# Strassen's seven products for all pairs of projection tiles of a hybrid attention layer

## What is computed

```python
h = jnp.einsum('bsd,de->bse', x, w_in) + b_in            # 1024 x 1024 @ 1024 x 5376
q_a, k_a, v_a, gate_a, q_b, k_b, v_b, gate_b, mg_a, mg_b = jnp.split(h, split_points, axis=-1)
o_a = swa_sink_attention(rope(q_a), rope(k_a), v_a, sinks) * silu(gate_a)   # 8 heads, window of 2 chunks of 64
o_b = stick_breaking_attention(q_b, k_b, v_b) * silu(gate_b)                # 8 heads, causal, 128-query blocks
merged = sigmoid(mg_a) * (o_a @ w_up_a) + sigmoid(mg_b) * (o_b @ w_up_b)
out = layer_norm(alpha * x + merged @ w_out, ln_g, ln_b)
```

## Time and profile before

| what | us |
| --- | --- |
| median of 3 runs (lowest, highest) | 805.31 (802.58, 805.39) |
| the profiled execution, its own time | 805.12 |
| its span | 803.4 |
| PE busy | 782.4 |
| DVE busy | 425.3 |
| ACT busy | 371.9 |
| POOL busy | 241.8 |

### The profile page before, as it was taken

One profiled execution on the slowest core, in us unless ns is written; L12 is line 12 of the kernel. 1 busy time (PEld: TensorE's weight loads), 2 busy tenths in 40 slices (PEclk: granted clock), 3 DMA queues, 4 the chain that ended last, 5 costly groups with the idle time before them and its releaser, 6 DMA issues.

```text
span 803.4 us, 10295 instructions
## 1 busy us (share of the span) xinstructions
PE 782.4 (97%) x4088; PEld 617.3 (77%) x4088; DVE 425.3 (53%) x518; ACT 371.9 (46%) x628; POOL 241.8 (30%) x177
## 2 busy tenths in 40 slices
PE   7999999999999999999999999989999999999996
PEld 6888778778677777777777777768887888888884
DVE  6377555534445445554444667934166367670543
ACT  7688555552555545454554544543546012140221
POOL 0221111112433222322223333455453122200592
PEclk9999999999999999999999999989999999999999
DMA  9231000011001000000004123241515533441261
GB/s 318 76 106 53 26 27 27 27 53 53 27 28 51 27 28 27 26 29 26 28 27 157 56 102 131 80 159 52 170 40 187 206 129 119 173 157 53 93 209 66
DMA packets 25199, 68.85 MB, mean 86 GB/s; under 512 B 2880, under 2 KB 2880, under 8 KB 25152
## 3 DMA queue, kind: packets, MB, share of 16 engines
q1 hardware_dynamic: 25152, 68.20, 24.6%
HBM read 54.55 MB, written 12.58 MB: 84 GB/s over the span
## 4 chain that ended last, share of the span: by engine, by line
PE 89%; DVE 5%; ACT 2%; issue 1%; DMA 1%; POOL 0%; SPq 0%; DVEq 0%; POOLq 0%
PE ps L168 25%; PE ps L170 24%; PE ps L169 24%; PE ps L1415 5%; PE ps L1444 4%; PE ps L1431 4%; PE ps L1360 2%; PE ps L1343 1%; PE ps L1371 1%; DVE xs L1111 1%; DVE t_ops L1094 1%; DMA x_f<-in_xt 1%; DMA raw<-in_w 1%; DVE keep_big L1052 1%; DVE x_lo L1094 0%
## 5 line engine op out<-in xcount | busy, mean ns | idle before, releaser
L168 PE MATMUL ps<-x_hi,w_hi 128*128 128x512 f32 x640 | 262.6, 410 | 6.2 <-DVE x_lo L1094 3.3
L170 PE MATMUL ps<-x_hi,w_lo 128*128 128x512 f32 x640 | 252.3, 394 | 0.0
L169 PE MATMUL ps<-x_lo,w_hi 128*128 128x512 f32 x640 | 251.3, 393 | 0.0
L489 POOL TENSOR_TENSOR w_lo<-raw,w_hi 128x1024 fp32r<-128x1024 f32 x33 | 80.4, 2436 | 296.6 <-ACT w_hi L556 296.6
L168 PEld LDWEIGHTS ps<-x_hi,w_hi 128*128 128x128 f32 x640 | 121.2, 189 | 45.7 <-issue 19.2
L170 PEld LDWEIGHTS ps<-x_hi,w_lo 128*128 128x128 f32 x640 | 121.1, 189 | 27.0
L169 PEld LDWEIGHTS ps<-x_lo,w_hi 128*128 128x128 f32 x640 | 121.7, 190 | 22.3
L1052 DVE TENSOR_TENSOR_SCAN keep_big<-keep_big 128x1025 f32<-128x1025 f32 (+3 forms) x32 | 61.4, 1962 | 63.4 <-POOL keep_big L504 63.4
L168 PE MATMUL ps<-t_ops,w_hi 128*128 128x512 f32 x136 | 53.9, 396 | 1.7 <-POOL w_lo L495 1.7
L170 PE MATMUL ps<-t_ops,w_lo 128*128 128x512 f32 x136 | 53.4, 392 | 0.0
L169 PE MATMUL ps<-t_ops,w_hi 128*128 128x512 f32 x136 | 52.9, 389 | 0.0
(11 more groups left out here) (171 smaller groups left out, 1247.7 us busy)
## 6 DMA issues: line engine op xcount, KB each, us to landing
raw<-in_w SPq DMA_DIRECT2D x42, 512.0 KB, 3.3
sig_d<-sig_m SPq DMA_DIRECT2D x32, 256.0 KB, 2.2
sig_m<-sig_d SPq DMA_DIRECT2D x16, 512.0 KB, 4.2
o_t<-in_xt SPq DMA_DIRECT2D x16, 256.0 KB, 6.2
raw<-in_xn SPq DMA_DIRECT2D x8, 512.0 KB, 3.6
out<-o_t SPq DMA_DIRECT2D x16, 256.0 KB, 2.1
raw_c<-in_w SPq DMA_DIRECT2D x7, 512.0 KB, 4.7
v_t<-in_w SPq DMA_DIRECT2D x7, 512.0 KB, 4.7
```

What stands on the lines that cost most here:

```text
L168: pe.matmul(out, w_hi, x_hi, start=first, stop=False, skip_group_check=goes_on)
L169: pe.matmul(out, w_hi, x_lo, start=False, stop=False, skip_group_check=goes_on)
L170: return pe.matmul(out, w_lo, x_hi, start=False, stop=last, skip_group_check=goes_on)
L489: pool.tensor_tensor(w_lo[:, at, :], raws[raw_buffer(n)], w_hi[:, at, :].bitcast(F32), ALU.subtract).then_inc(lo_done, 1)
```

## The change

Two tiles (K_A, V_A) stay whole; the other 40 are 20 pairs, and each pair is made by seven products (12 matmuls each) in the order 1, 2, 6, 3, 7, 5, 4 (positions 0 to 6). The sums of x are made right after x is split. Two PSUM banks hold products, by turns: positions 0, 2, 4, 6 accumulate in one bank and ACT copies it out after each; positions 1, 3, 5 start afresh in the other and DVE adds them to the blocks straight from PSUM (5 to two blocks). A product waits for the reading of the product two before it. In the window stage an iteration has one product in place of a quarter tile; a step of the stick-breaking stage has seven half products (42 matmuls) in place of 48. Window scores are plain float32 on 64 rows, four matmuls per chunk, in two banks by turns; q is rotated by swapping quarters of its partitions with DMAs. The transposes for the next pair's values go from the last step of four to the first step of the next four. The keep scans write in a tile which also takes the transposed weights. Outputs of both attentions go through DRAM and come back in one go after the steps, and the gates of the window attention are multiplied in the last stage. Warm-up transposes go from 16 to 24, with 16 more after the first three matmuls.

```diff
+ORDER = (1, 2, 6, 3, 7, 5, 4)
+NP = len(ORDER)
+WINDOW_0 = 14
+STEP_0 = 42
+def slots(s):
+    at = 2 * STEP_0 + NP * s
+    return (at, at + 1), (at + 2,), (at + 3, at + 4), (at + 5,), (at + 6,)
+def completed(s, slot):
+    return [i // 2 for i in slots(s)[slot] if i % 2]
+def next_parts(q):
+    return {0: (q + 3, q + 4), 5: (), 6: (q + 3,)}.get(q % NP, (q + 4,)) if q < N_PRODUCTS - 4 else ()
...
 # PE
+            def half_product(u):
+                q, part = u // 2, u % 2
+                which = ORDER[q % NP]
+                if part == 0:
+                    pe.wait_ge(part_lo, q + 1)
+                    if q < 2:
+                        pe.wait_ge(k_cos, q + 1)
+                        pe.wait_ge(swapped, 4 * (q + 1))
+                    else:
+                        read_i, read_pos = (q - 2) // NP, (q - 2) % NP
+                        if read_pos % 2:
+                            pe.wait_ge(block_sum, 4 * read_i + (1, 2, 4)[read_pos // 2])
+                        else:
+                            pe.wait_ge(bank_read, 4 * read_i + read_pos // 2 + 1)
...
             for s in range(STEPS):
                 scores(s, False)
-                fill(s, (0, 1))
+                fill(s, 0)
                 if s > 0:
                     turn(s - 1, True, (0, 1))
-                fill(s, (2, 3))
+                fill(s, 1)
                 if s > 0:
                     values(s - 1, True)
                 scores(s, True)
-                fill(s, (4, 5))
-                if s % 4 == 3 and s < STEPS - 1:
-                    turn_values(s // 4 + 1)
+                fill(s, 2)
+                if s % 4 == 0 and s > 0:
+                    turn_values(s // 4)
                 turn(s, False, (0, 1))
-                fill(s, (6,))
+                fill(s, 3)
                 turn(s, False, (2, 3))
-                fill(s, (7,))
+                fill(s, 4)
                 values(s, False)
...
 # ACT
+            def after(q):
+                i, pos = q // NP, q % NP
+                read_bank(q)
+                if i >= MG_PAIR:
+                    for b in {2: (0,), 6: (1, 2)}.get(pos, ()):
+                        block_sigmoid(i, b)
...
+                for n in next_parts(q):
+                    part_high(n)
...
+            keys_swap(0)
+            value_half(0)
+            sum_hi(1)
+            sum_hi(3)
+            part_high(0)
+            part_high(1)
+            sum_hi(2)
+            keys_swap(1)
+            value_half(1)
+            part_high(2)
+            sum_hi(4)
...
             for s in range(STEPS):
                 betas(s, False)
+                for q in completed(s, 0):
+                    after(q)
                 if s > 0:
-                    turned_blocks(s - 1, True)
-                fill_half(s, 0)
+                    turned_blocks(s - 1, True, (0, 1))
+                for q in completed(s, 1):
+                    after(q)
                 betas(s, True)
...
 # DVE
+            def after(q):
+                i, pos = q // NP, q % NP
+                if i - 1 in Q_PAIRS and pos < 3:
+                    rotate_block(i - 1, pos + 1)
+                for k in {1: (0,), 3: (1,), 5: (2, 3)}.get(pos, ()):
+                    add_block(i, k)
+                if pos in (4, 5) and i + 1 < N_PAIRS:
+                    weight_sums(i + 1, pos == 4)
...
+            sum_raw(1)
+            sum_raw(3)
+            sum_raw(2)
...
+            rotate_keys(0)
+            sum_lo(1)
+            sum_lo(3)
+            sum_lo(2)
+            weight_sums(0, True)
+            rotate_keys(1)
+            weight_sums(0, False)
+            sum_lo(4)
...
             for s in range(STEPS):
                 break_sticks(s, False)
                 if s > 0:
                     gated_out(s - 1, True)
+                for place in range(2):
+                    for q in completed(s, place):
+                        after(q)
                 break_sticks(s, True)
...
 # SP
+            for q in range(STEP_0 + NP * STEPS // 2, N_PRODUCTS):
...
+                after(q)
+                if q == STEP_0 + NP * STEPS // 2 + 1:
+                    outputs_back()
+                    load_w(UP_0 + 2)
+                    load_w(UP_0 + 3)
+                    gate_back(0)
```

More of the change, by code:

```diff
@@ L677, in _, with gate_b_sigmoid @@
-            rope_hi(*before)
-            window_group(3)
+            def gate_b_sigmoid(p):
+                i = pair_vg(p)
+                for h in range(2):
+                    wait_block(act, i, 1, h)
+                    if p == 0 and h == 0:
+                        for k in range(2):
+                            act.wait_ge(oa_out[k], 16 * NCHUNK // 4)
+                    if p > 0:
+                        act.wait_ge(gate_set, 2 * (p - 1) + h + 1)
+                    act.activation(sig_g[:, h, :], o_b[p % 2][:, half(h)], ACT.Sigmoid).then_inc(gate_sig, 1)
@@ new lines, in _ @@
+            first_weights_hi(0, 0)
+            for h in range(2):
+                for k in range(KT):
+                    if h == 0 and k == 2:
+                        first_weights_hi(0, 1)
+                    act.wait_ge(x_in[KT * h + k], 16)
+                    act.activation(x_hi[:, k, half(h)], xr[:, k, half(h)], ACT.Copy).then_inc(x_hi_done, 1)
+                if h == 0:
+                    first_weights_hi(1, 0)
+                    first_weights_hi(1, 1)
+            act.wait_ge(const_in, 32)
@@ L872, in _ @@
-            block_sigmoid(last, 7)
+                if s % 4 == 0 and s > 0:
+                    gate_b_sigmoid(s // 4)
+                for q in completed(s, 2):
+                    after(q)
+                if s % 4 == 0 and s > 0:
+                    turned_values(s // 4)
+                turned_blocks(s, False, (0, 1))
+                for q in completed(s, 3):
+                    after(q)
+                turned_blocks(s, False, (2, 3))
+                for q in completed(s, 4):
+                    after(q)
@@ L873, in _ @@
+            after(STEP_0 + NP * STEPS // 2)
+            turned_blocks(STEPS - 1, True, (0, 1))
+            for q in range(STEP_0 + NP * STEPS // 2 + 1, N_PRODUCTS):
+                after(q)
             weight_hi(UP_0 + 1)
@@ L1184, in merge @@
+                if s % 4 == 0 and s > 0:
+                    gate_b_product(s // 4)
+                for place in range(2, 5):
+                    for q in completed(s, place):
+                        after(q)
+                gated_out(s, False)
+            after(STEP_0 + NP * STEPS // 2)
+            after(STEP_0 + NP * STEPS // 2 + 1)
+            gated_out(STEPS - 1, True)
+            for q in range(STEP_0 + NP * STEPS // 2 + 2, N_PRODUCTS):
+                after(q)
             def merge(j):
@@ L1321, in _ @@
+            for q in range(WINDOW_0 + 3):
+                product(q)
+                if NP < q <= NP + 4:
+                    i = q - NP - 1
+                    if i == 0:
+                        pe.wait_ge(v_read, 2)
                     bank = t_bank(i)
```

1353 lines of the change are left out of this document (621 added, 732 removed).

## The result

The kernel after takes 864.6 us (median of 4 runs, 862.7 to 865.2) where the kernel before takes 805.4: a ratio of 1.073, 95% interval 1.071 to 1.076. It is slower, as forecast, but by 59 us and not by 10; 865 lies outside the range that ended at 842.

The account below looks back on a forecast made before the run. PE's executed work plus its waits was taken to bound the kernel. Against 805.1 us, -38.1 - 3 - 7.3 + 12 + 3 + 37.3 (steps) + 6 = +9.9, so 815 us; 787 to 842 for 8 in 10.

Parts of the forecast that it names:

- POOL's low parts are hidden: In the steps: POOL's 3.5 low parts of 1.53 us per step, in place of one of 2.44, cost nothing.
- old start of the products: Sums of x under the products go, with waits of 1.32 and 3.29 us and a 2.7 us slow stretch: -7.3 us.
- new start: At the start, products 1 and 3 wait for DVE, with slow clock behind: +12 us, bounds 8 and 15.
- rotation and window: Rotations fill DVE over products 3 to 16, and window-stage adds and sums crowd one iteration: +3 us, bounds 0 and 10.
- steps: waits: PE's waits in the steps for DVE's adds, ACT's copies and step 0's transposes: +27.3 us together.
- steps: clock: Slow matmuls behind the five step waits over 3 us, 2.7 us each, less what they take off later waits: +10 us.
- last stage: After the steps, a weight load behind ten 512 KB loads makes PE wait some 4 us, plus 2 for clock: +6 us.
- the forecast's four waits: In the steps: 4.0 us in 1, 5, 9, 13; 0.6 in steps like 7; 1.4 in 4, 8, 12; 0.5 in steps like 6.
- this rival: DVE and POOL hold each other up in each step: 18 us in the steps, 5 in the window, 838 us; chance 0.16.
- the clock stays: The waits come but the clock stays at 2.4 GHz: 802 to 803 us, no change; chance 0.13.
- all waits hidden: All waits are hidden by work not seen moved: 772 us; chance 0.05.
- the add of 3 is not late: In steps 1, 5, 9, 13 position 3's add ends before PE arrives: 4 x (4.0 + 2.7) fall away, 788 us; chance 0.21.

Follow-up runs that it names:

- low_short: The kernel after with POOL making only 32 of 512 columns of each low part in the steps, all orders kept: 838.6 us, ratio 1.042.
- odd_only: The kernel after with the add of position 3 ahead of the big scans in odd steps, even steps unchanged: 833.7 us, ratio 1.034.
- six_edits: four_edits with a third order of DVE's start and ACT's copies of the small weights ahead of its part of the product: 789.6 us, ratio 0.980.
- burst_late: The kernel after with the seven 512 KB branch loads issued one product later, behind pair 15's second weight tile: 857.5 us, ratio 1.066.
- pool_cut: The kernel after with the small cut ahead of the low parts of the first two places on POOL: 848.2 us, ratio 1.055.
- gate_late: The kernel after with the window gates' products behind the adds of position 5 in the last product stage: 848.5 us, ratio 1.057.
- four_edits: The kernel after with adds ahead of scans, gate_late, burst_late, and the key-bank rotation earlier in DVE's start: 796.5 us, ratio 0.989.

## Why the prediction was wrong

The direction, the kind of loss and most of its places were right; the sum was 50 us short. Half of that is one step of the prediction, that POOL's low parts are hidden. By its own terms, with measured values from the windows and waits above:

| term | predicted | measured |
| --- | --- | --- |
| matmuls removed | -38.1 | -38.1 (168) |
| window scores | -3 | -4.6 (0.71 us in place of 1.00, 16 times) |
| old start of the products | -7.3 | -7.3 |
| new start | +12 | +14 (product 3 at 51.26 for an ideal 37.3) |
| rotation and window | +3 | about +8 |
| steps: waits | +27.3 | +46 |
| steps: clock | +10 | +17.5 |
| last stage | +6 | +26 (19 waits, 7 clock) |
| sum | +9.9 | +61 (the span grew by 60.1) |

The steps can be summed again with POOL out of the way. In low_short their idle time is 30.6 us, 28.9 more than before the change (forecast 27.3). Their busy time is 13.65 less where 102 instructions fewer are worth 23.2, so 9.5 us is clock (forecast 10). The steps come out 15.3 us longer than before the change, where the forecast's +37.3 - 21.8 is 15.5. So all else that the prediction put in the steps holds, and what the kernel after loses beyond it, 25 us, is POOL.

- **Right.** Product 1 waited 10.23 us (7 to 11) and started at 43.76 (43). The odd steps waited 4.69 to 4.72 us for the add behind scans and product (4.0), four times. Steps 4, 8 and 12 waited 1.22 for ACT's copies (1.4), the other even ones 0.57 (0.5). One wait stood soon after the steps for an add behind a weight sum that waited for a DMA. odd_only, six_edits and burst_late confirm the last three by their removal.
- **The step that failed: "POOL's low parts are hidden".** I let them cost nothing, as most would miss DVE's product. They weren't: its two low parts come free some 2 us after the big scans start (231.03 against 228.83 in step 1), run beside scans and product, and hold up what stands behind them in POOL's order. That makes the odd wait 4.7 instead of 3.9 and the wait of step 3 1.42 instead of 0.59. It also starts the even steps' chain (low parts, small cut, small scans, add), four waits of 2.2 to 2.5 us, about 9, that stood nowhere in the sum. low_short, in which the forecast's four waits stand to 0.2 us, and pool_cut show it. With the slow clock that followed, it cost 25 us. I held this rival at 0.16 and priced it at 18 us in the steps, as longer instructions only and not as a queue.
- **The even steps' add of position 1 was never placed.** I followed the add of 3 in the odd steps and took the even ones to have only ACT's wait. With POOL out of the way it is not late (low_short), so this cost nothing by itself; but left unplaced, it is where POOL's queue came out.
- **The last stage was mis-sized: 20 us of the 50.** The burst cost a wait of 7.9 us and not 4. And of the gates' products I wrote that they "are counted in it", without placing them: 2.44 us in front of adds that had no slack, four times. gate_late took 15 us out. The 2.75 us at pair 19 were in no term.
- **The clock was charged by too narrow a rule.** I charged it to waits over 3 us alone. In the steps of low_short, where nearly all the others are under 1.3 us, that gave the right size. But in the kernel after waits of 1.97, 2.21 and 2.25 us have 7 or 8 matmuls at 0.43 us behind them too, and transposes and values in such a stretch are slow as well. The profile of before had it: behind the wait of 1.48 us that the earlier trace rows names, eight matmuls in a row start 0.427 us apart, while the prediction weighs only the wait of 1.32, which has none. The first and the last of the eight:

```profile
87.42 0.63 PE L168 MATMUL ps<-x_hi,w_hi 128*128 128x512 f32 x1
...
90.40 0.56 PE L169 MATMUL ps<-x_lo,w_hi 128*128 128x512 f32 x1
```

- In all, over the steps, 46 us of waits brought 17.5 of slow work, and 15.8 of it came back when the adds were first.
- The rival "the clock stays" is refuted, and so is "all waits hidden". The one on the faster side, that the add of 3 is not late, is what odd_only makes true by an edit. It priced this at 27 us (4 x 6.7); 31 were measured, the four waits of 1.4 us among them.

The change was not a bad one: its 38 us are there, and in six_edits 16 of them are kept. What it cost came mostly from where the new instructions were written into three queues.

## What to carry to other kernels

When a change makes TensorE wait for a short instruction of another engine, write that instruction into the other engine's queue ahead of whatever long work starts at the same time; an add of 0.67 us behind scans and product cost 31 us over the eight odd steps. When placing new work by timelines, place every new instruction of every queue in both kinds of step: the ones taken as "hidden" or "counted in it" made most of this error. Leaving one engine's work out, as low_short does, is a way to see what that engine alone costs. In a kernel like this one, count idle time of TensorE at about 1.5 times its length (1.2 to 1.7 in the edits here), and retest each edit in company, since an order that gained 16 us alone lost 5 beside others.

## What the runs showed of the hardware

- The granted clock fell behind waits as short as 1.48 us (in the kernel before, at 85.72) and 1.97 (in the kernel after, at 73.67): 1.2 GHz for eight 512-wide matmuls each. It did not behind each of that size: the waits of 2.25 us at 611.99 and of 2.20 at 430.95 have no slow matmul behind them. Nor is it fixed by the kernel: at the start, where gate_late has the same instructions as the kernel after, waits of 1.95 and 2.22 us have none behind them in its profile, and waits of 1.97 and 2.21 have 7 or 8 each in the other, so that gate_late reaches the window scores 2.8 us sooner. What decides it no run here tells. In four_edits and six_edits, which have no wait over 3.3 us after 66 us, only 4 and 6 starts 0.43 us apart are left after that time, where the kernel after has 89.
- Two low parts on POOL beside a DVE scan and product of two SBUF operands took 5.2 to 6.5 us in place of 3.1, in steps 0, 1 and 2. The scans themselves were not longer; the product was, by 0.8 us. So at this place POOL paid most of it, and through its queue PE did.
- A short POOL instruction that met a long one of DVE lasted until that one ended: in low_short 1.95 us for a low part of 0.25 beside a scan, and 2.19 for a cut of 0.41 beside the product. The product kept its 2.03 us there.
